# Attention of a hybrid block: unnormalised exponentials, three rounded value products, head outputs scaled by rows of inverse sums that go through DRAM

## The chip, the cores and the metric

One core of a Trainium2 chip runs the whole program. The metric is device microseconds of one execution, from start to end; lower is better. All inputs lie in DRAM as float32, and the output is float32.

## What is computed

The reference is one layer of a network on 512 tokens of width 1024 with a context of 256 more: a feed-forward sublayer, a mixer (a gated delta rule over 8 heads in both directions, and a softmax attention with 8 query heads over 2 key and value heads), and a second feed-forward sublayer. The change touches the attention alone, for 512 queries over 768 keys, 128 wide:

```python
def _attend(q, k, v):
    b, lq = q.shape[:2]
    qg = q.reshape(b, lq, ATTN_KV_HEADS, ATTN_GROUP, ATTN_DH)
    s = jnp.einsum('bqkgd,bskd->bkgqs', qg, k).astype(jnp.float32) * (ATTN_DH ** -0.5)
    p = jax.nn.softmax(s, axis=-1).astype(v.dtype)
    o = jnp.einsum('bkgqs,bskd->bqkgd', p, v)
    return o.reshape(b, lq, ATTN_Q)
```

## The kernel before, in words

The program is written by hand for each engine. Every engine runs its own list in order: SP loads weights, GpSimd (POOL) does some sums and DMAs, ScalarE (ACT), VectorE (DVE) and TensorE (PE) do the rest. Engines wait for each other by counting semaphores, `wait_ge` in front of an instruction and `then_inc` behind it. Nothing reorders the lists, so the order of the work is the order of the code.

Most matrix products are made as three products of operands that are rounded to the format fp32r: a value x is kept as x_hi (rounded, copied by ACT) and x_lo = x - x_hi (subtracted by DVE), and hi x hi, hi x lo and lo x hi are added up in PSUM. The feed-forward layers, the projections and the attention's scores are made so. The attention's value products are plain fp32 products.

PSUM has 8 banks of 512 columns. In the attention banks 4 to 7 hold scores (two banks for even tiles, two for odd ones), banks 0 and 1 the transposed probabilities of one tile, and banks 2 and 3 the outputs of an even and an odd head.

The attention goes over 32 tiles, i = 4n + t: head n of 8, and in it the block t of 128 queries. Their steps are interleaved:

- PE (lines 3161 to 3204): `scores(i + 2)`, six products of 384 columns, once the exponential of tile i is done; then six transposes of tile i, 128 keys each, of the normalised probabilities; then `weigh(i - 1)`, six fp32 products of 128 columns.
- DVE (lines 2407 to 2428): the maximum of tile i (L2417), its scaling by -1/sqrt(128) (L2420), then `normalise(i - 1)`: a reciprocal of the row's sum (L2410) and the scaling of 768 columns (L2412).
- ACT (lines 1509 to 1536): the exponential of tile i with its sum (L1522), then `evac_pt(i - 1)`, the copy of the 768 transposed columns to SBUF (L1512), and for t = 2 the copy of the last head's output (L1518).

Into the first tiles falls other work: the last query item is rotated and split (`item_rotate`, `item_hi`, `item_low`, lines 2307 to 2329 and 1445), and the values are turned by PE (L3146) and copied by ACT (L1505). At the end PE waits for all 8 heads (L3207) and goes on with the projections of the delta rule, `dn_gemm(0, 0)` to `dn_gemm(0, 2)` (L3407). POOL also waits for all heads (L854), then clears `d_s` and `d_up` (L856, L858); ACT and DVE wait for that before their part of the delta rule (L1695, L2436).

## Time and profile before

| what | value |
|---|---|
| time, median of 3 runs | 1834.33 us (1832.84 to 1838.05) |
| the profiled execution's own time | 1840.07 us |
| its span, first to last instruction | 1838.4 us |
| mean granted clock of TensorE | 0.996 |
| busy: PE, DVE, ACT, POOL | 97%, 67%, 52%, 22% of the span |
| attention, first reduction to first product behind it | 687.42 to 787.74 us |

All rows further down come from the profiled execution. A row of the timeline gives start and length in us, engine, line of the kernel, operation, output and inputs by the program's names, and in brackets how long the engine idled before it and who released it. Rows of the same kind that follow each other are merged (x6: six instructions). PE's matmuls overlap: the start of the next one tells the pace, not the length. `PE` rows of an fp32 product count twice (x12 for six products).

### The profile page before, as it was taken

What the parts mean: (1) busy time and instruction counts of PE and PEld (TensorE: products, weight loads), DVE (VectorE), ACT (ScalarE), POOL (GpSimd) and SP (SyncE); (2) the same over time, 40 slices, a digit from 0 to 9 for tenths busy, and PEclk for the clock granted to TensorE, in tenths of its full rate; (3) what the DMA queues carried; (4) which work ended last, traced back from release to release, by engine and by line L of the source; (5) the groups of instructions that cost most, each with busy time, mean ns of one, the idle gap of its engine ahead of it and who ended that gap; (6) DMA issues with size and microseconds to landing.
All of it is one profiled execution on the core that took longest, in us unless ns stands there. A gap on an engine that the chain in (4) does not pass through costs nothing.

```text
span 1838.4 us, 31419 instructions
## 1 busy us (share of the span) xinstructions
PE 1783.9 (97%) x11197; PEld 1657.6 (90%) x11197; DVE 1234.2 (67%) x2451; ACT 953.1 (52%) x1910; POOL 402.9 (22%) x296
## 2 busy tenths in 40 slices
PE   8899999999998999999999999999999999999997
PEld 5899999999997889999999999987889888898997
DVE  7768787868757666556777877765334675375576
ACT  6534242424446656565666666654223675464453
POOL 0714141313200120023232213310000052341330
PEclk9999999999999999999999999999999999999999
DMA  8133324454241430021222221122224112223232
GB/s 330 64 131 125 129 104 159 165 185 159 86 161 41 137 109 26 1 64 47 69 77 65 77 77 52 46 63 80 102 92 172 47 69 104 81 92 116 92 116 69
DMA packets 85142, 182.88 MB, mean 99 GB/s; under 512 B 33572, under 2 KB 42916, under 8 KB 84912
## 3 DMA queue, kind: packets, MB, share of 16 engines
q1 hardware_dynamic: 79584, 167.45, 26.4%
q0 software_dynamic: 3280, 13.95, 2.3%
q8 instruction: 63, 1.03, 0.2%
q10 hardware_dynamic: 2176, 0.13, 0.1%
q14 instruction: 39, 0.32, 0.1%
HBM read 169.91 MB, written 7.39 MB: 96 GB/s over the span
## 4 chain that ended last, share of the span: by engine, by line
PE 78%; DVE 7%; ACT 5%; issue 4%; POOL 2%; DMA 2%; SPq 2%; ACTq 0%; DVEq 0%; POOLq 0%
PE ps L2744 54%; PE ps L2955 15%; PE ps L3042 3%; PE ps L2748 3%; DMA raw<-W 1%; PE ps L3199 1%; ACT e_hi L1294 1%; DVE e_lo L2103 1%; SPq L748 1%; PE ps L3366 1%; PE ps L3328 1%; ACT ps L1279 1%; DVE ps L2145 1%; DVE w_lo L1993 0%; PE ps L3238 0%
## 5 line engine op out<-in xcount | busy, mean ns | idle before, releaser
L2744 PE MATMUL ps<-h_hi,w_hi 128*128 128x384 f32 (+2 forms) x720 | 240.9, 372 | 8.0 <-DVE h_lo L1879 3.4
L2744 PE MATMUL ps<-h_lo,w_hi 128*128 128x384 f32 (+2 forms) x720 | 237.7, 362 | 0.0
L2744 PE MATMUL ps<-h_hi,w_lo 128*128 128x384 f32 (+2 forms) x720 | 228.8, 357 | 0.0
L1809 DVE TENSOR_TENSOR w_lo<-raw,w_hi 128x1024 fp32r<-128x1024 f32 (+1 forms) x98 | 124.5, 1271 | 120.1 <-ACT w_hi L966 120.0
L966 ACT ACTIVATE w_hi<-raw 128x1024 fp32r<-128x1024 f32 (+1 forms) x106 | 111.3, 1050 | 146.8 <-PE ps L2744 144.9
L2744 PEld LDWEIGHTS ps<-h_hi,w_hi 128*128 128x128 f32 x720 | 130.8, 189 | 29.1 <-DVE h_lo L1879 8.0
L2744 PEld LDWEIGHTS ps<-h_lo,w_hi 128*128 128x128 f32 x720 | 133.5, 189 | 12.7 <-issue 1.2
L2744 PEld LDWEIGHTS ps<-h_hi,w_lo 128*128 128x128 f32 x720 | 133.3, 188 | 12.6
L2744 PE MATMUL ps<-g_hi,w_hi 128*128 128x384 f32 (+2 forms) x444 | 132.9, 346 | 0.8 <-DVE w_lo L1809 0.5
L2744 PE MATMUL ps<-g_lo,w_hi 128*128 128x384 f32 (+2 forms) x444 | 131.7, 343 | 0.0
L2744 PE MATMUL ps<-g_hi,w_lo 128*128 128x384 f32 (+2 forms) x444 | 131.7, 343 | 0.0
L3042 PE MATMUL ps<-f_hi,e_hi 128*128 128x256 f32 x356 | 102.1, 287 | 7.9 <-ACT f_pb L1338 3.9
L2955 PE MATMUL ps<-h_lo,w_hi 128*128 128x384 f32 x320 | 107.0, 334 | 2.2 <-ACT pb L1224 2.2
L2955 PE MATMUL ps<-h_hi,w_hi 128*128 128x384 f32 x320 | 107.3, 335 | 0.4 <-DVE ps L2033 0.3
L2955 PE MATMUL ps<-h_hi,w_lo 128*128 128x384 f32 x320 | 106.9, 334 | 0.0
L2955 PE MATMUL ps<-x_lo,w_hi 128*128 128x384 f32 x320 | 106.9, 334 | 0.0
L3042 PE MATMUL ps<-f_hi,e_lo 128*128 128x256 f32 x356 | 100.6, 283 | 0.0
L815 POOL TENSOR_TENSOR sums<-raw 128x512 f32<-128x512 f32 x20 | 28.9, 1444 | 278.6 <-DVE w_lo L1993 181.7
L2744 PEld LDWEIGHTS ps<-g_hi,w_hi 128*128 128x128 f32 x444 | 81.5, 188 | 7.4 <-DVE Y L2091 1.0
L2744 PEld LDWEIGHTS ps<-g_hi,w_lo 128*128 128x128 f32 x444 | 81.7, 188 | 5.0
L2744 PEld LDWEIGHTS ps<-g_lo,w_hi 128*128 128x128 f32 x444 | 81.7, 188 | 5.0
L1993 DVE TENSOR_TENSOR w_lo<-sums,w_hi 128x512 fp32r<-128x512 f32 x80 | 59.9, 753 | 33.8 <-ACT w_hi L1184 33.1
(478 smaller groups left out, 5112.9 us busy)
## 6 DMA issues: line engine op xcount, KB each, us to landing
raw<-W SPq DMA_DIRECT2D x221, 512.0 KB, 3.3
w_mod<-WMOD SPq DMA_DIRECT2D x68, 512.0 KB, 3.4
g_row<-g_rows POOLq DMA_DIRECT2D x8, 768.0 KB, 4.5
X<-XT SPq DMA_DIRECT2D x4, 768.0 KB, 7.1
d_matrices<-d_l SPq DMA_DIRECT2D x8, 384.0 KB, 2.8
a_sw<-i_n POOLq DMA_DIRECT2D x40, 64.0 KB, 1.9
w_first<-WMOD SPq DMA_DIRECT2D x4, 512.0 KB, 11.0
X<-XT SPq DMA_DIRECT2D x1, 2048.0 KB, 14.1
```

Of the source, the lines that this page charges most:

```text
L748: sp.dma_start(d_s[lv][r:r + b, :, col:col + b], d_l[r:r + b, 0, :, col:col + b]).then_inc(s("d_levels"), 16)
L815: g.tensor_tensor(s1[:], b1, b2, ALU.add).then_inc(s("s_add"), 1)
L966: a.activation(hi, src, ACT.Copy).then_inc(s("w_hi"), 1)
L1279: a.activation(copy_bank(pos), weight_part2(q, pos), ACT.Copy)
L1294: a.activation(slot2(True, q, pos), weight_part2(q, pos), ACT.Copy).then_inc(s("u_hi"), 1)
L1809: v.tensor_tensor(lo, src, hi.bitcast(F32), ALU.subtract).then_inc(s("w_split"), 1)
L1993: v.tensor_tensor(slot_of(w_lo, n, None), weight_part(q, pos), slot_of(w_hi, n, None).bitcast(F32), ALU.subtract)\
L2103: v.tensor_tensor(slot2(False, q, pos), src, slot2(True, q, pos).bitcast(F32), ALU.subtract).then_inc(s("u_lo"), 1)
L2744: return pe.matmul(out, lhsT, rhs, start=start, stop=stop)
L2748: return pe.matmul(out, lhsT, rhs, start=False, stop=True, skip_group_check=True)
L2955: last = pe.matmul(out_, slot_of((w_hi, w_hi, w_lo)[i], n + pos, k), (hi, lo, hi)[i][pos][:, k], start=pos in (A11, A12, S3) and k == 0 an ...
L3042: last = pe.matmul(out_, w[i][:, k], (hi, lo, hi)[i][:, k], start=pos in (A11, A12, S3) and k == 0 and i == 0, stop=True, skip_group_check ...
```

## The change

Five things change, all in the attention.

1. The exponentials are not normalised. PE transposes them as they come, three in bank 0 and three in bank 1, each bank with its own semaphore step.
2. ACT copies each bank's 384 columns as `p_hi` (`evac_hi`), and DVE subtracts that from PSUM into `p_lo` (`evac_low`). The values are split likewise: `v_hi` by ACT, `v_lo` by DVE (`value_low`).
3. The value products are made for two tiles together: a block `weigh(p, b)` handles the three key blocks of bank b for the pair p of tiles, with three fp32r products of 256 columns each. In tile i PE does `weigh(i // 2 - 1, i % 2)`, and after the last tile two blocks more.
4. After a head's four tiles DVE makes the reciprocals of its 4 x 128 sums (`recip`). POOL stores them as a row of 512 numbers in DRAM and loads that row into all 128 partitions (`a_r`); DVE multiplies the head's output by it (`out_head`), three tiles later.
5. PE waits for seven heads only before `dn_gemm(0, 0)`, and for the eighth before `dn_gemm(0, 2)`.

The diff, cut to its core:

```diff
         a_kc = at("a_kc", 204, [HKV, CTX])
-        a_v = at("a_v", 187, [NCH, HKV, P])
+        v_hi = at("v_hi", 187, [NCH, HKV, P], F32R)
+        v_lo = at("v_lo", 174, [NCH, HKV, P], F32R)
         i_raw = [at(f"i_raw{i}", 147 + 16 * i, [T]) for i in range(2)]
...
         a_p = at("a_p", 200, [2, T])
-        a_pt = [at("a_pt0", 147, [NCH, SEQ]), at("a_pt1", 159, [NCH, SEQ])]
-        a_m = at("a_m", 183, [3, 4])
+        p_hi = [at(f"p_hi{i}", 147 + 12 * i, [NCH, 2 * P], F32R) for i in range(2)]
+        p_lo = [at(f"p_lo{i}", 153 + 12 * i, [NCH, 2 * P], F32R) for i in range(2)]
+        a_m = at("a_m", 183, [4, 8])
+        a_r = [at(f"a_r{i}", 193 + 2 * i, [SEQ]) for i in range(2)]
         ba = at("ba", 184, [T])
...
             return ps[:, b, 0:(CTX, SEQ)[seg]]
+        def turned(b):
+            return ps[:, b, 0:3 * P].rearrange("p (c n) -> p c n", c=3)
+        def turned_to(t, i, b):
+            return t[i // 2 % 2][:, 3 * b:3 * b + 3, P * (i % 2):P * (i % 2) + P]
+        def head_bank(n):
+            return ps[:, 3 - n % 2, :]
         def solver_out(i):
...
             g.wait_ge(s("cb_loaded"), 16)
+            for n in range(H):
+                g.wait_ge(s("at_sum"), 2 * N_ITEM + n + 1)
+                g.dma_start(DL[0, 4 * n:4 * n + 4, :].rearrange("t q -> q t"), a_m[:, 3, 4 * (n % 2):4 * (n % 2) + 4], allow_slow_non_contiguous=True).then_inc(s("rows_stored"), 16)
+                g.wait_ge(s("rows_stored"), 32 * n + 32)
+                g.wait_ge(s("o_at"), n)
+                g.dma_start(a_r[n % 2][:], DL[0:1, 4 * n:4 * n + 4, :].rearrange("b t q -> b (t q)").to_broadcast([P, SEQ])).then_inc(s("rows_stored"), 16)
+                g.wait_ge(s("rows_stored"), 32 * n + 48)
             g.wait_ge(s("o_at"), H + 1)
...
                 a.wait_ge(s("at_vt"), j + 1)
-                a.activation(a_v[:, :, j, :].rearrange("p (b c) n -> p b c n", b=2),
+                a.activation(v_hi[:, :, j, :].rearrange("p (b c) n -> p b c n", b=2),
                              ps[:, 2 * j:2 * j + 2, 0:384].rearrange("p b (c n) -> p b c n", c=3), ACT.Copy).then_inc(s("at_vc"), 1)
-            def evac_pt(i):
-                a.wait_ge(s("at_tr"), i + 1)
-                t = i % 4
-                a.activation(a_pt[i // 4 % 2][:, :, P * t:P * t + P].rearrange("p (b c) n -> p b c n", b=2),
-                             ps[:, 0:2, 0:384].rearrange("p b (c n) -> p b c n", c=3), ACT.Copy)\
-                 .then_inc(s("at_pt"), 1)
-            def out_head(n):
-                a.wait_ge(s("at_pv"), n + 1)
-                a.activation(o_at[:, n, :], ps[:, 2 + n % 2, 0:SEQ], ACT.Copy).then_inc(s("o_at"), 1)
+            def evac_hi(i):
+                if i % 2 == 0 and i >= 4:
+                    a.wait_ge(s("at_pv"), i // 2 - 1)
+                if i == 2:
+                    a.wait_ge(s("at_rot"), N_ITEM)
+                for b in range(2):
+                    a.wait_ge(s("at_tr"), 2 * i + b + 1)
+                    a.activation(turned_to(p_hi, i, b), turned(b), ACT.Copy).then_inc(s("at_pt"), 1)
             for i in range(4 * H):
-                t = i % 4
                 a.wait_ge(s("at_max"), 2 * i + 2)
+                if i >= 8 and i % 4 == 0:
+                    a.wait_ge(s("at_sum"), 2 * N_ITEM + i // 4 - 1)
                 a.activation(a_p[:, i % 2, :].rearrange("p (b n) -> p b n", b=2),
                              ps[:, 4 + 2 * (i % 2):6 + 2 * (i % 2), 0:384],
-                             ACT.Exp, bias=a_m[:, 1, t:t + 1], scale=DH ** -0.5,
-                             accum_out=a_m[:, 2, t:t + 1]).then_inc(s("at_p"), 1)
+                             ACT.Exp, bias=a_m[:, 1, i % 8:i % 8 + 1], scale=DH ** -0.5,
+                             accum_out=a_m[:, 2, i % 8:i % 8 + 1]).then_inc(s("at_p"), 1)
                 if i == 0:
                     for j in range(HKV):
                         value_tokens(j)
                 if i:
-                    evac_pt(i - 1)
+                    evac_hi(i - 1)
                 if i == 1:
                     item_hi(N_ITEM - 1)
-                if i >= 4 and t == 2:
-                    out_head(i // 4 - 1)
-            evac_pt(4 * H - 1)
-            out_head(H - 1)
+            evac_hi(4 * H - 1)
             def take(b):
...
                     v.tensor_copy(g_out[0:96, :], ps[0:96, 6, 0:P]).then_inc(s("gates_v"), 1)
-            def normalise(i):
-                t = i % 4
-                v.wait_ge(s("at_p"), i + 1)
-                v.reciprocal(a_m[:, 2, t:t + 1], a_m[:, 2, t:t + 1]).then_inc(s("at_pn"), 1)
-                v.wait_ge(s("at_pn"), 2 * i + 1)
-                v.tensor_scalar(a_p[:, i % 2, :], a_p[:, i % 2, :], a_m[:, 2, t:t + 1], None, ALU.mult)\
-                 .then_inc(s("at_pn"), 1)
+            def value_low(j):
+                v.wait_ge(s("at_vc"), 2 * j + 1)
+                v.wait_ge(s("at_vt"), HKV)
+                v.tensor_tensor(v_lo[:, :, j, :].rearrange("p (b c) n -> p b c n", b=2),
+                                ps[:, 2 * j:2 * j + 2, 0:384].rearrange("p b (c n) -> p b c n", c=3),
+                                v_hi[:, :, j, :].rearrange("p (b c) n -> p b c n", b=2).bitcast(F32), ALU.subtract).then_inc(s("at_vc"), 1)
+            def evac_low(i):
+                for b in range(2):
+                    v.wait_ge(s("at_pt"), 2 * i + b + 1)
+                    v.tensor_tensor(turned_to(p_lo, i, b), turned(b), turned_to(p_hi, i, b).bitcast(F32), ALU.subtract).then_inc(s("at_pl"), 1)
+            def recip(n):
+                v.wait_ge(s("at_p"), 4 * n + 4)
+                if n >= 2:
+                    v.wait_ge(s("rows_stored"), 32 * (n - 2) + 32)
+                c = slice(4 * (n % 2), 4 * (n % 2) + 4)
+                v.reciprocal(a_m[:, 3, c], a_m[:, 2, c]).then_inc(s("at_sum"), 1)
+            def out_head(n):
+                v.wait_ge(s("at_pv"), 2 * n + 2)
+                v.wait_ge(s("rows_stored"), 32 * n + 48)
+                v.tensor_tensor(o_at[:, n, :], head_bank(n), a_r[n % 2][:], ALU.mult).then_inc(s("o_at"), 1)
             for i in range(4 * H):
-                t = i % 4
+                c = i % 8
                 v.wait_ge(s("at_s"), i + 1)
-                v.tensor_reduce(out=a_m[:, 0, t:t + 1], in_=ps[:, 4 + 2 * (i % 2):6 + 2 * (i % 2), 0:384],
+                v.tensor_reduce(out=a_m[:, 0, c:c + 1], in_=ps[:, 4 + 2 * (i % 2):6 + 2 * (i % 2), 0:384],
                                 op=ALU.max, axis=AX.XY).then_inc(s("at_max"), 1)
                 v.wait_ge(s("at_max"), 2 * i + 1)
-                v.tensor_scalar(a_m[:, 1, t:t + 1], a_m[:, 0, t:t + 1], -DH ** -0.5, None, ALU.mult)\
+                v.tensor_scalar(a_m[:, 1, c:c + 1], a_m[:, 0, c:c + 1], -DH ** -0.5, None, ALU.mult)\
                  .then_inc(s("at_max"), 1)
+                if i == 0:
+                    for j in range(HKV):
+                        value_low(j)
                 if i:
-                    normalise(i - 1)
+                    evac_low(i - 1)
                 if i == 1:
                     item_rotate(N_ITEM - 1)
                 if i == 2:
                     item_low(N_ITEM - 1)
-            normalise(4 * H - 1)
+                if i and i % 4 == 0:
+                    recip(i // 4 - 1)
+                if i > 4 and i % 4 == 3:
+                    out_head(i // 4 - 1)
+            recip(H - 1)
+            evac_low(4 * H - 1)
+            out_head(H - 1)
             def bc(x):
...
                 last.then_inc(s("at_s"), 1)
-            def weigh(i):
-                n, t = i // 4, i % 4
-                pe.wait_ge(s("at_pt"), i + 1)
-                if t == 0 and n >= 2:
+            def turn(i):
+                pe.wait_ge(s("at_p"), i + 1)
+                for b in range(2):
+                    if i:
+                        pe.wait_ge(s("at_pl"), 2 * i - 1 + b)
+                    for c in range(3):
+                        last = pe.transpose(ps[:, b, P * c:P * c + P], a_p[:, i % 2, P * (3 * b + c):P * (3 * b + c + 1)], ident)
+                    last.then_inc(s("at_tr"), 1)
+            def weigh(p_, b):
+                n = p_ // 2
+                pe.wait_ge(s("at_pl"), 4 * p_ + 3 + b)
+                if p_ % 2 == 0 and b == 0:
                     pe.wait_ge(s("o_at"), n)
-                for c in range(NCH):
-                    last = mm(ps[:, 2 + n % 2, P * t:P * t + P], a_v[:, c, n // 4], a_pt[n % 2][:, c, P * t:P * t + P],
-                              c == 0, c == NCH - 1)
-                if t == 3:
+                for c in range(3 * b, 3 * b + 3):
+                    for i, (v_, x) in enumerate(((v_hi, p_hi), (v_hi, p_lo), (v_lo, p_hi))):
+                        last = mm(head_bank(n)[:, 2 * P * (p_ % 2):2 * P * (p_ % 2) + 2 * P], v_[:, c, n // 4], x[p_ % 2][:, c],
+                                  c == 0 and i == 0, c == NCH - 1 and i == 2)
+                if b:
                     last.then_inc(s("at_pv"), 1)
...
                     scores(i + 2)
-                pe.wait_ge(s("at_pn"), 2 * i + 2)
-                if i:
-                    pe.wait_ge(s("at_pt"), i)
                 if i == 0:
-                    pe.wait_ge(s("at_vc"), HKV)
-                for c in range(NCH):
-                    last = pe.transpose(ps[:, c // 3, P * (c % 3):P * (c % 3) + P],
-                                        a_p[:, i % 2, P * c:P * c + P], ident)
-                last.then_inc(s("at_tr"), 1)
-                if i:
-                    weigh(i - 1)
-            weigh(4 * H - 1)
-            pe.wait_ge(s("o_at"), H + 1)
+                    pe.wait_ge(s("at_vc"), 2 * HKV)
+                turn(i)
+                if i >= 2:
+                    weigh(i // 2 - 1, i % 2)
+            for b in range(2):
+                weigh(2 * H - 1, b)
+            pe.wait_ge(s("o_at"), H)
             def merge_gemm(it, j):
...
             dn_gemm(0, 1)
+            pe.wait_ge(s("o_at"), H + 1)
             dn_gemm(0, 2)
```

DVE's order in the middle of the attention, before (`a_m` holds maxima, scaled maxima and sums, `a_p` the probabilities, `ps` is PSUM):

```order
L2417 TENSOR_REDUCE a_m<-ps 128x1 [waits at_s]
L2420 TENSOR_SCALAR a_m<-a_m 128x1 [waits at_max]
L2410 RECIPROCAL a_m<-a_m 128x1 [waits at_p]
L2412 TENSOR_SCALAR a_p<-a_p,a_m 128x768 [waits at_pn]
L2417 TENSOR_REDUCE a_m<-ps 128x1 [waits at_s]
```

Now, at the end of one head and the start of the next:

```order
L2449 TENSOR_REDUCE a_m<-ps 128x1 [waits at_s]
L2452 TENSOR_SCALAR a_m<-a_m 128x1 [waits at_max]
L2433 TENSOR_TENSOR p_lo_141<-ps,p_hi_139 128x3x128 [waits at_pt] x2
L2445 TENSOR_TENSOR o_at<-ps,a_r_143 128x512 [waits rows_stored,at_pv]
L2449 TENSOR_REDUCE a_m<-ps 128x1 [waits at_s]
L2452 TENSOR_SCALAR a_m<-a_m 128x1 [waits at_max]
L2433 TENSOR_TENSOR p_lo_141<-ps,p_hi_139 128x3x128 [waits at_pt] x2
L2440 RECIPROCAL a_m<-a_m 128x4 [waits at_p]
```

The reciprocal and scaling that waited for an exponential (`at_p`) have given way to two subtractions that wait for ACT's copies (`at_pt`), ahead of the next reduction. The head's product also waits for POOL's DMA (`rows_stored`).

ACT's order at the same place, before:

```order
L1522 ACTIVATE a_p,a_m<-ps,a_m 128x768 [waits at_max]
L1512 ACTIVATE a_pt_138<-ps 128x6x128 [waits at_tr]
L1518 ACTIVATE o_at<-ps 128x512 [waits at_pv]
L1522 ACTIVATE a_p,a_m<-ps,a_m 128x768 [waits at_max]
L1512 ACTIVATE a_pt_138<-ps 128x6x128 [waits at_tr]
```

and now:

```order
L1541 ACTIVATE a_p,a_m<-ps,a_m 128x768 [waits at_max]
L1536 ACTIVATE p_hi_139<-ps 128x3x128 [waits at_tr] x2
L1541 ACTIVATE a_p,a_m<-ps,a_m 128x768 [waits at_max]
L1536 ACTIVATE p_hi_138<-ps 128x3x128 [waits at_tr,at_pv]
L1536 ACTIVATE p_hi_138<-ps 128x3x128 [waits at_tr]
```

The copies of a tile still stand behind the exponential of the next one; there are two instead of one, and the head's copy is gone.

## Rows read from the trace of the kernel before

**Rows 1.** The page: busy time of each engine
```profile
PE 1783.9 (97%) x11197; PEld 1657.6 (90%) x11197; DVE 1234.2 (67%) x2451; ACT 953.1 (52%) x1910; POOL 402.9 (22%) x296
```

**Rows 2.** Busy times of three tiles' time: us, then busy us (x instructions) of each engine
```profile
700.00:709.12 9.12, 9.12 (x74) 9.02 (x74) 5.41 (x12) 5.24 (x9) 0.00 (x0) 1.00 0.00 0
```

**Rows 3.** Who waited for whom, 686 to 788 us: total, times, longest
```profile
DVE a_m L2417 <- PE ps L2744: 32.5, 28, 1.2
```

**Rows 4.** Timeline, one tile: start us, us, engine line op, out<-in, count
```profile
723.53 0.59 PE L2744 MATMUL ps<-k_hi,q_hi 128*128 128x384 f32 x2
...
724.66 0.82 PE L3199 MATMUL ps<-ca,a_p 128*128 128x128 f32 x6
...
724.86 0.96 DVE L2417 TENSOR_REDUCE a_m<-ps 128x1 f32<-128x768 f32 x1 [1.17 <-PE ps L2744]
...
725.31 1.50 PE L2744 MATMUL ps<-a_pt,a_v 128*128 128x128 f32 x12
...
725.85 0.16 DVE L2420 TENSOR_SCALAR a_m<-a_m 128x1 f32<-128x1 f32 x1
...
726.22 0.90 ACT L1522 ACTIVATE a_p<-ps,a_m 128x768 f32<-128x768 f32 x1
...
726.57 0.59 PE L2744 MATMUL ps<-k_hi,q_hi 128*128 128x384 f32 x2
```

**Rows 5.** Timeline, the first tiles of the attention
```profile
687.42 0.95 DVE L2417 TENSOR_REDUCE a_m<-ps 128x1 f32<-128x768 f32 x1
...
688.59 0.90 ACT L1522 ACTIVATE a_p<-ps,a_m 128x768 f32<-128x768 f32 x1 [1.59 <-DVE a_m L2420]
...
689.48 1.50 ACT L1505 ACTIVATE a_v<-ps 128x768 f32<-128x768 f32 x2
...
690.35 0.68 DVE L2315 TENSOR_TENSOR a_t<-i_n,cb 128x512 f32<-128x512 f32 x1
...
690.95 0.69 DVE L2317 TENSOR_TENSOR a_t<-a_sw,cb 128x512 f32<-128x512 f32 x1
...
692.28 0.95 DVE L2417 TENSOR_REDUCE a_m<-ps 128x1 f32<-128x768 f32 x1
```

**Rows 6.** One line's instructions: duration ns min/median/max
```profile
L976 ACT ACTIVATE v_raw<-ps x4: 470/476/483, 679.1 to 686.5; 128x384 f32<-128x384 f32 x4
```

**Rows 7.** Timeline, elsewhere: two subtractions on DVE; two 256-column products
```profile
100.65 0.55 DVE L2026 TENSOR_TENSOR pa<-ps,pa 128x384 f32<-128x384 f32 x1
...
101.12 0.95 DVE L2019 TENSOR_TENSOR g_lo<-ps,g_hi 128x768 fp32r<-128x768 f32 x1
...
101.99 0.68 DVE L1993 TENSOR_TENSOR w_lo<-raw,w_hi 128x512 fp32r<-128x512 f32 x1
...
1640.24 0.28 PE L3042 MATMUL ps<-f_hi,e_lo 128*128 128x256 f32 x1
...
1640.36 0.28 PE L3042 MATMUL ps<-f_hi,e_hi 128*128 128x256 f32 x1
```

**Rows 8.** Timeline, the end of the attention and what follows
```profile
779.58 0.96 DVE L2417 TENSOR_REDUCE a_m<-ps 128x1 f32<-128x768 f32 x1 [1.17 <-PE ps L2744]
...
787.74 0.50 PE L2744 MATMUL ps<-h_hi,w_hi 128*128 128x512 f32 x1 [0.69 <-ACT o_at L1518]
...
789.42 0.74 POOL L858 MEMSET d_up<- 128x772 f32 x1
...
793.53 0.60 ACT L1699 ACTIVATE d_up<-ps 128x512 f32<-128x512 f32 x1 [3.04 <-PE ps L2744]
```

**Rows 9.** DMA issues of the page: KB each, us to landing
```profile
g_row<-g_rows POOLq DMA_DIRECT2D x8, 768.0 KB, 4.5
...
d_b<-d_matrices SPq DMA_DIRECT2D x8, 48.0 KB, 2.0
```

**Rows 10.** Timeline, slack in the first head of the delta rule
```profile
811.17 0.63 DVE L2459 TENSOR_SCALAR d_c<-d_up,hn 128x770 f32<-128x770 f32 x1 [1.28 <-ACT d_up L1546]
```

**Rows 11.** Busy times in the second FFN, columns as in rows 2, then PEclk
```profile
1660.00:1680.00 20.00, 17.87 (x141) 16.97 (x140) 14.89 (x24) 11.82 (x25) 4.74 (x4) 1.00 0.40 135
```

## Prediction

> **What bounds the kernel now.** I read the page first. It shows a kernel in which TensorE's matmuls fill the span [rows 1], which says nothing yet of the stage that changes. The windows in the middle of the attention are plainer: 9.12 us of 9.12 are busy on PE, 5.41 on DVE and 5.24 on ACT, at a granted clock of 1.00, the 2.4 GHz level [rows 2]. 9.12 us are three tiles (a tile is 128 queries of one head; there are 32), so one takes 3.04. The waits agree: DVE's reduction waits for PE's scores before 28 of the 32 tiles, 32.5 us in all [rows 3], and no wait of PE of that size stands there. The timeline splits the 3.04 us [rows 4]: scores from 723.53 to 724.66 (1.13), six transposes to 725.31 (0.65), value products to 726.57 (1.26). PE is the bound, and DVE and ACT each idle over 3 of every 9 us. A product saved on PE pays only while DVE and ACT can follow. Busy times alone do not tell that: the order in their queues does.
>
> **The change on PE.** Six fp32 value products of a tile (twelve PE instructions, 1.26 us) become nine products of 256 columns. Such products follow each other every 0.12 us (1640.24 to 1640.36) [rows 7], so 9 x 0.12 = 1.08. PE's tile costs 1.13 + 0.65 + 1.08 = 2.86, 0.18 less; that is 5.8 us in 32 tiles, if PE stays the bound.
>
> **The change on DVE and ACT.** DVE loses a scaling of 768 columns and a reciprocal, and gets two subtractions of 384 columns per tile, one reciprocal and one product of 512 columns per head. ACT's one copy of 768 becomes two of 384, and its head copy goes. As busy time both still fit under 2.86 us. But look at what waits for what in the new order:
> - DVE, tile i: reduce i, scale i, then the two subtractions of tile i-1, which wait for ACT's copies of tile i-1;
> - ACT, tile i: exponential i, which waits for scale i, and only then the copies of tile i-1;
> - DVE's reduce i+1 stands behind those subtractions.
>
> So reduce i, scale i, exponential i, copies i-1, subtractions i-1, reduce i+1 is one closed chain through two queues, and each tile runs it once. Before, DVE's second half of tile i needed only exponential i-1, long done, and the copies were in nobody's way. The chain's price:
> - reduce start to exponential start, 687.42 to 688.59: 1.17 [rows 5];
> - exponential start to the next ACT instruction, 688.59 to 689.48: 0.89 [rows 5];
> - first copy of 384 columns from PSUM, 0.476 [rows 6], and 0.04 for the handover (a reduce ends at 724.86 + 0.96 = 725.82 and the scale that waits for its semaphore starts at 725.85 [rows 4]; I round up): 0.52. The second copy runs beside the first subtraction;
> - two subtractions: after one of 384 columns the next DVE instruction starts 0.47 later (100.65 to 101.12), although the instruction lasts 0.55 [rows 7]: 0.94.
>
> Sum 3.52 us per tile, over PE's 2.86 and over the present 3.04. PE is not in the chain: scores i+1 start when exponential i-1 is done, 1.13 + 0.65 later transposes i-1 are issued, and ACT comes to copy them only 3.52 + 0.89 after the start of exponential i-1.
>
> **One place where the skill differs.** The pair of rows above has the next instruction start 0.08 us before the subtraction's end [rows 7], and I count the start distance. The Trainium skill, VectorE: DVE Perf Modes, section "The TRN2 errata — SBUF-src ops pay a fixed extra latency per instruction", gives an fp32 tensor_tensor (N+151)/0.96 ns, 557 ns at 384 columns, and says that this latency is exposed between instructions; by it the chain would be 2 x 0.09 longer and the result an estimated 5.4 us later. This trace agrees with the 0.55 as a duration and not as a distance.
>
> **Per head** the chain also carries, between subtractions and next reduce, the reciprocal (0.15, like the small scaling of rows 4) and the head's product of 512 columns (0.60, from 690.35 to 690.95) [rows 5].
>
> **The sum**, from reduce 0, which nothing earlier moves:
> - Reduce 0 to 1: exponential 0 starts at 1.17, the value copies at 2.06; the second subtraction of v_lo starts at 2.91 + 0.87 = 3.78 (the first waits for one copy, 0.8; 768 columns take 0.87, 101.12 to 101.99 [rows 7]) and reduce 1 at 4.65.
> - Reduce 1 to 2: the chain, 3.52, and the rotation of the last item, 690.35 to 692.28, 1.93 [rows 5]: at 10.10.
> - Reduce 2 to 3: 3.52 and q_lo, 0.60: at 14.2.
> - Reduce 3 to 31: 28 x 3.52 = 98.6, seven reciprocals 1.05, six head products 3.6: at 117.4.
> - Before, reduce 31 came 779.58 - 687.42 = 92.2 after reduce 0 [rows 5, 8]. That is +25.2.
> - Tail: before, 8.16 from reduce 31 to the first product of the delta rule at 787.74 [rows 8]. Now the subtractions of tile 30 end at 3.6, the last transposes are issued by 4.0, three blocks of nine products take 3.24, and the wait is for the seventh head alone: 7.2. That is -0.9.
>
> **Sum +24.3 us.** The profiled execution took 1840.07 us (span 1838.4), 5.7 above the median of 1834.33; the difference is applied to the median: 1858.6.
>
> **What I cost at nothing, and its cover.** The row of inverse sums goes out to DRAM and back. DVE needs it three reductions after the reciprocal, 3 x 3.52 = 10.6 us later. The trace has no store of 4-byte pieces. From below: 768 pieces of 64 B landed in 2.0 us [rows 9], and a 256 KB load lies between that and the 768 KB one of 4.5 [rows 9], so 2.0 + 2.6 = 4.6. From above: both at twice the first and at the second, 4.0 + 4.5 = 8.5, plus up to 1 us of issue. I take 6, since counts of pieces resemble the first row. All are below 10.6, so nothing waits; from there on each microsecond counts in seven heads. For the last head the cover is PE's: the first two blocks of the delta rule use no bank of that head; the first takes 5.8 us (787.74 to 793.53) [rows 8], the second has 48 products of 384 columns at 1.13 / 6 [rows 4], 9 us. POOL's clearing of d_up now follows this product: reciprocal done at 4.3, row at 10.3, product at 11.1, and as before 2.5 us to the clearing's end (789.42 + 0.74, 2.4 after the start at 787.74): 13.5, or 6.3 after PE's start. ACT first needs it 5.8 after (793.53) [rows 8]. These 0.5 us vanish in the slack further on, where DVE idled 1.28 [rows 10]; at a trip of 9.5 us some 2 us would remain.
>
> **Rivals.**
> 1. *PE stays the bound, no slowdown.* If the handovers overlapped enough for the chain to fall from 3.52 + 0.19 (the head's share) to 2.86, the stage would be 14.2 + 28 x 2.86 = 94.3 against 92.2, less 0.9: +1.2 us, 1835.5. For it: DVE and ACT are busy only 60% now. Against it: each link is a measured duration of this stage or its shape, and 0.85 us per tile would have to vanish. It decides (less than 5.5 us over before) from about 3.0 down, the head's share included.
> 2. *The row comes late.* With a trip of 15 us, DVE waits 4.4 us in front of seven products: +31, 1889. For it: 512 separate 4-byte writes per head, of which there is no row. Against: [rows 9].
> 3. *TensorE's clock falls.* PE would be busy 2.86 of 3.7 us instead of all the time. At the 1.2 GHz level its tile is 5.7 us and becomes the bound: 32 x (5.7 - 3.04) = +85, 1919. Against it: with 17.87 of 20 us busy, in pieces, the clock stood at 1.00 [rows 11]; a share of 77% has no row. The Trainium skill, TensorE: Matmul & The Clock Gate, part 1, says that idling throttles the array to 1.2 GHz; no run here shows how much idling that takes.
> 4. *The change does not use its new products*: excluded, since the diff's loops over plain numbers make all 18 per pair of tiles.
>
> **How the numbers follow.** The closed chain 0.87; rival 1, 0.04; rival 2, 0.06; rival 3, 0.03. The prediction is 1858.6 us. Low end: each of the two subtractions 0.07 shorter and the run at the fast end (1832.84), -4.5 - 1.5: 1852. High end: subtractions at their full 0.55 (+4.9), the late clearing (+2), waits for two semaphores and the slow end of the runs (+3): 1869. About 0.3% is what a measurement of this kernel can tell from no change. Slower 0.93, within 0.3% 0.04 (rival 1), faster 0.03 (rival 1 with cheaper products than rows 7 show).
>
> **What would show it.** Right: reductions about 3.5 us apart, 4.1 where a head's product lies between; ACT's copies starting as soon as the exponential lets them, not when the transposes end; PE idle some 0.8 us per tile in front of scores; the inverse rows landing before DVE asks. Wrong: PE busy throughout (rival 1), DVE waiting on a DMA at the head's product (rival 2), PEclk near 0.5 (rival 3).

## The result, and the profile after

The changed kernel takes **1897.74 us** (median of six runs, 1896.54 to 1900.15) against 1834.91 for the kernel before in the same comparison (1832.84 to 1839.77): ratio 1.0339, 95% interval 1.0324 to 1.0354, or 62.8 us slower. Forecast were 1858.6 us and a range of 1852 to 1869. The direction was right; of the increase I had seen 24 us of 63, and the time lies far outside the range. The profiled execution of the changed kernel took 1897.12 us.

The page of the changed kernel. First its head line and the busy times, to be held against [rows 1]; then the slices with TensorE's granted clock, the chain of work that ended last (shares of the span), and two of the DMA issues (engine's queue, count, KB each, median us from issue to landing):

```profile
span 1895.1 us, 31340 instructions
...
PE 1794.0 (95%) x11101; PEld 1662.9 (88%) x11101; DVE 1245.7 (66%) x2469; ACT 950.6 (50%) x1934; POOL 413.0 (22%) x312
...
PE   8899999999998987678999999999999999999997
...
PEclk9999999999999998899999999999999999999999
...
PE 63%; DVE 10%; DMA 9%; ACT 7%; issue 5%; SPq 3%; POOL 2%; DVEq 0%; ACTq 0%; POOLq 0%
...
a_r<-d_matrices POOLq DMA_DIRECT2D x8, 256.0 KB, 4.7
...
d_matrices<-a_m POOLq DMA_DIRECT2D x8, 2.0 KB, 8.8
```

The busy times of DVE, ACT and POOL hardly moved. What is new sits in three places: PE's busy slices fall to 6 to 8 tenths in the attention, the clock row has two 8s there, and 9% of the chain now runs through DMA, where it was 2%. The two DMA rows give the reason away at once. The row of inverse sums, 2 KB, takes 8.8 us to be stored, nearly twice as long as the 256 KB that are read back. The next view, who waited for whom from 680 to 860 us in the changed kernel (total, times, longest), says who pays:

```profile
ACT a_p L1541 <- DVE a_m L2452: 84.4, 32, 7.3
...
POOL a_r L872 <- DMA d_matrices<-a_m: 67.7, 8, 9.2
DVE p_lo L2433 <- ACT p_hi L1536: 46.0, 31, 2.5
DVE o_at L2445 <- DMA a_r<-d_matrices: 41.1, 8, 13.6
...
PE ps L2785 <- ACT a_p L1541: 34.9, 13, 5.8
```

[Rows 3] had DVE waiting for PE before 28 tiles. Nothing of that is left. DVE now waits for ACT's copies in 31 tiles (the chain that was forecast, 1.5 us each) and for the row from DRAM at all eight head products: 41.1 us in all, 13.6 of them for the last head, so 27.5 for the seven others, 3.9 each. The forecast had no wait there.

One head on DVE, in the timeline of the changed kernel (start, length, what it waited for):

```profile
747.49 0.17 DVE L2440 RECIPROCAL a_m<-a_m 128x4 f32<-128x4 f32 x1
747.57 0.93 DVE L2449 TENSOR_REDUCE a_m<-ps 128x1 f32<-128x768 f32 x1
...
751.06 0.95 DVE L2449 TENSOR_REDUCE a_m<-ps 128x1 f32<-128x768 f32 x1
...
754.60 0.95 DVE L2449 TENSOR_REDUCE a_m<-ps 128x1 f32<-128x768 f32 x1
...
757.18 1.02 DVE L2433 TENSOR_TENSOR p_lo<-ps,p_hi 128x384 fp32r<-128x384 f32 x2 [1.44 <-ACT p_hi L1536]
763.00 0.69 DVE L2445 TENSOR_TENSOR o_at<-ps,a_r 128x512 f32<-128x512 f32 x1 [4.80 <-DMA a_r<-d_matrices]
763.61 0.95 DVE L2449 TENSOR_REDUCE a_m<-ps 128x1 f32<-128x768 f32 x1
```

and the same trip on POOL:

```profile
748.21 0.76 POOL L869 DMA_DIRECT2D d_matrices<-a_m  x1 [8.97 <-DVE a_m L2440]
757.44 0.54 POOL L872 DMA_DIRECT2D a_r<-d_matrices  x1 [8.47 <-DMA d_matrices<-a_m]
```

The reductions are 3.49 and 3.54 us apart where no wait for a row lies between them; 3.52 was forecast. The reciprocal starts at 747.49, the store is issued at 748.21 and has landed by 757.4, the load is issued at 757.44, and the product can start at 763.00: a trip of 15.5 us. Without the wait the product would have started at 763.00 - 4.80 = 758.20, so the cover was 10.7 us, and 10.6 was forecast. Everything on DVE stands behind that product, so 4.8 us of waiting delay the reduction at 763.61, and with it the exponential, the scores and PE.

Where the seven waits end, the last head begins its own:

```profile
837.91 0.17 DVE L2440 RECIPROCAL a_m<-a_m 128x4 f32<-128x4 f32 x1
...
852.60 0.69 DVE L2445 TENSOR_TENSOR o_at<-ps,a_r 128x512 f32<-128x512 f32 x1 [13.62 <-DMA a_r<-d_matrices]
...
855.01 0.73 POOL L879 MEMSET d_up<- 128x772 f32 x1
...
855.78 0.31 ACT L1712 ACTIVATE ones_r<-ca 128x128 fp32r<-128x128 f32 x1 [21.01 <-POOL d_up L879]
...
857.62 1.23 DVE L1825 TENSOR_TENSOR w_lo<-raw,w_hi 128x1024 fp32r<-128x1024 f32 x1 [1.24 <-ACT w_hi L987]
```

Product, POOL's clearing of `d_up`, ACT's first instructions and DVE's next weights follow one another; PE, which began the delta rule at 840.82, then waits 4.15 us at 858.95 for those weights. ACT's start of the delta rule was forecast 6.3 us after PE's; it came 855.78 - 840.82 = 15.0 after.

The first reduction of the attention stands where it stood, at 687.46 (before 687.42 [rows 5]). The first product of the delta rule has gone from 787.74 [rows 8] to 840.82. So 53.0 us of the increase lie between the two. DVE's copy of the delta rule's first head shows what follows, first in the kernel before and then now:

```profile
864.27 0.69 DVE L2475 COPY d_o<-ps 128x512 f32<-128x512 f32 x1 [2.19 <-PE ps L2748]
```
```profile
840.82 0.40 PE L2785 MATMUL ps<-h_hi,w_hi 128*128 128x512 f32 x1
...
925.10 0.69 DVE L2516 COPY d_o<-ps 128x512 f32<-128x512 f32 x1 [2.19 <-PE ps L2789]
```

It came 76.5 us after the first product and now comes 84.3 after it, which adds 7.7: 60.7 up to there. The medians are 62.8 apart. The two profiled executions as a whole differ by only 57.0 (1897.12 and 1840.07), because behind this copy that of the kernel before takes 4.1 us longer (974.1 against 970.0) in code that the change does not touch. So the 60.7 are an account of the stage, and the whole agrees with them within a few us, not better.

The granted clock is the last thing to read. Busy time by windows of the changed kernel (us, then PE, PEld, DVE, ACT and POOL busy with their counts, granted clock, DMA share, GB/s):

```profile
686.00:726.00 40.00, 26.79 (x170) 24.55 (x168) 22.14 (x40) 16.66 (x36) 1.90 (x3) 0.91 0.14 40
726.00:766.00 40.00, 27.22 (x169) 26.15 (x170) 18.51 (x38) 15.26 (x35) 2.60 (x4) 0.86 0.09 14
766.00:806.00 40.00, 29.47 (x178) 27.92 (x179) 19.93 (x41) 14.80 (x35) 3.35 (x5) 0.84 0.07 14
```

and PE's first instructions after one of the waits, in the timeline:

```profile
746.19 1.01 PE L2785 MATMUL ps<-k_hi,q_hi 128*128 128x384 f32 x2 [4.75 <-ACT a_p L1541]
...
748.27 1.48 PE L3218 MATMUL ps<-ca,a_p 128*128 128x128 f32 x6
```

PE is busy two thirds to three quarters of the time at 0.84 to 0.91 of full clock, where [rows 2] have 1.00. After an idle time of 4.75 us its two score products take 1.01 us instead of 0.59 and the six transposes 1.48 instead of 0.82 [rows 4]. From 746.2 to 750 us the granted clock is 0.50, the lower level of 1.2 GHz.

### The profile page after: what moved, and what is told of

The parts are those of the page before. It is cut to its first block, busy times and chain, and to the rows that moved or that the text cites. A ratio compares the mean times of both kernels' runs of the same rounds, so it can differ in the third digit from the quotient of the medians.

```text
span 1895.1 us, 31340 instructions
## 1 busy us (share of the span) xinstructions
PE 1794.0 (95%) x11101; PEld 1662.9 (88%) x11101; DVE 1245.7 (66%) x2469; ACT 950.6 (50%) x1934; POOL 413.0 (22%) x312
## 3 DMA queue, kind: packets, MB, share of 16 engines
q8 instruction: 62, 1.02, 0.2%
## 4 chain that ended last, share of the span: by engine, by line
PE 63%; DVE 10%; DMA 9%; ACT 7%; issue 5%; SPq 3%; POOL 2%; DVEq 0%; ACTq 0%; POOLq 0%
PE ps L2785 43%; PE ps L2996 14%; DMA d_matrices<-a_m 4%; PE ps L2789 3%; SPq L761 2%; DMA a_r<-d_matrices 2%; PE ps L3083 2%; DMA d_xc<-d_b 1%; DMA raw<-W 1%; ACT e_hi L1315 1%; DVE e_lo L2119 1%; DMA d_matrices<-d_l 1%; PE ps L3412 1%; ACT ps L1300 1%; ACT d_qu L1625 1%
```

## The experiments

After the result the working theory was: the chain costs what was forecast, the trip's excess over its cover costs seven times some 4 us, and the last head the rest. The rivals: that the slower clock or the DMA traffic, and not the wait, holds the heads up; that the missing time sits elsewhere; and, for the store, that the queue and not the size of its pieces makes it slow.

**e1_no_row: the trip taken out.** POOL fills both row buffers with 1.0 once, and the heads stay unnormalised. DVE's products stay where they are.

```diff
-            for n in range(H):
-                g.wait_ge(s("at_sum"), 2 * N_ITEM + n + 1)
-                g.dma_start(DL[...].rearrange("t q -> q t"), a_m[...])
...
+            g.wait_ge(s("at_sum"), 2 * N_ITEM + 1)
+            for n in range(2):
+                g.memset(a_r[n][:], 1.0).then_inc(s("row_set"), 1)
...
-                v.wait_ge(s("rows_stored"), 32 * n + 48)
+                v.wait_ge(s("row_set"), 2)
```

> Leaves out: the rows of inverse sums do not go through DRAM and are not used; POOL fills the two row buffers with 1.0 once, and the product with the head's output stays, so that every engine's instructions are as in the change, only the trip is gone. The profile of the change shows reductions 3.54 us apart between the head products and DVE idle 4.0 us before seven of them for the DMA. Theory A (two separate costs: the closed chain through ACT and DVE, about 24 us; and the trip of 15 us against a cover of 10.6, about 28 us in seven heads and 8 us behind the last head): 1835 + 24 = 1859, chain still 3.54 us per tile, no wait for a DMA, clock 1.00. Rival B (TensorE's fallen clock, 0.84 to 0.91 in the stage, is what lengthens it, and the trip only coincides): over 1875, and the clock stays under 1. Rival C (the chain exists only because the waits let the engines fall out of step): about 1836.

Measured: 1862.83 us (1861.21 to 1864.48; ratio 1.0142, interval 1.0125 to 1.0159), against 1835.84 for the kernel before in this comparison: +27.0. Four tiles of its timeline on DVE:

```profile
736.65 0.95 DVE L2443 TENSOR_REDUCE a_m<-ps 128x1 f32<-128x768 f32 x1
...
740.25 0.93 DVE L2443 TENSOR_REDUCE a_m<-ps 128x1 f32<-128x768 f32 x1
...
743.74 0.94 DVE L2443 TENSOR_REDUCE a_m<-ps 128x1 f32<-128x768 f32 x1
...
747.25 0.95 DVE L2443 TENSOR_REDUCE a_m<-ps 128x1 f32<-128x768 f32 x1
...
750.76 0.68 DVE L2439 TENSOR_TENSOR o_at<-ps,a_r 128x512 f32<-128x512 f32 x1
751.36 0.94 DVE L2443 TENSOR_REDUCE a_m<-ps 128x1 f32<-128x768 f32 x1
```

3.60, 3.49, 3.51 and, over the head product, 4.11: 14.71 us for a head of four tiles, where the prediction's own terms give 4 x 3.52 + 0.75 = 14.83. The clock is at 1.00 from 710 to 780 us. In the first tiles it is not: from 700 to 710 us it is 0.66. There the fourth and fifth steps between reductions take 4.74 and 3.97 us. PE has waited 4.19 us for `q_lo`, begins scores 4 at 702.26 at the lower level, and reaches the transposes of tile 2 only at 704.35, so ACT's copies wait 1.00 us for them. In its profiled execution the first reduction starts at 687.81 and the delta rule at 813.37, 125.6 us, where the kernel before took 787.74 - 687.42 = 100.3: 25.2 longer. Behind that nothing is left: the copy of the first head comes 76.7 us later, as before (76.5). So the chain is shown with its size, and the other 36 us of the increase hang on the trip. The profiled executions as a whole are 24.4 us apart (1864.48 and 1840.07), so they do not account for all of the medians' 27.0.

**e2_late: the head's product two tiles later, the trip unchanged.**

```diff
-                if i > 4 and i % 4 == 3:
-                    out_head(i // 4 - 1)
+                if i > 8 and i % 4 == 1:
+                    out_head(i // 4 - 2)
+            out_head(H - 2)
```

> The head's product and its wait for the row stand two tiles later in DVE's list (after tile 4n+9 instead of 4n+7), with the trip as it is; all is computed. Cover before the product: 5 chains of 3.54 = 17.7 us against a trip of 15. Theory A: the waits of seven heads vanish except at the last head and at the seventh, which now comes after the last reduction; the stage loses about 26 us, the delta rule's delay behind the last head (8 us) stays: about 1869 to 1873. Rival B (clock): over 1885. Rival C: as now, 1897, if DVE's wait was only idle time that another wait takes over.

Measured: 1871.47 us (1869.36 to 1876.05; 1.0200, 1.0180 to 1.0221). Its DMA rows and its two waits for the row:

```profile
a_r<-d_matrices POOLq DMA_DIRECT2D x8, 256.0 KB, 4.5
d_matrices<-a_m POOLq DMA_DIRECT2D x8, 2.0 KB, 8.4
```
```profile
ACT ones_r L1712 <- POOL d_up L879: 19.3, 1, 19.3
...
DVE o_at L2445 <- DMA a_r<-d_matrices: 15.7, 2, 13.1
```

The store is as slow as in the change, but DVE waits for it only twice: 2.6 us for the seventh head, whose product the edit could not put any later, and 13.1 for the last. The increase over the kernel before falls from 62.8 to 35.6 us, by 27, and the waits in the heads by 27.5 - 2.6 = 24.9. What is left over e1_no_row, 8.6 us, is the last two heads' trips, which this edit doesn't cover: the attention is 2.1 us longer (686.49 to 814.18) and the delta rule's first head comes 84.0 us after its start instead of 76.7, as in the change (84.3). The same traffic with a longer cover costs nothing in the heads: it was the wait.

**e3_store16: the store in pieces of 16 bytes.** Each partition's four inverse sums go out as they lie. The load is unchanged, so the row's order is no longer that of the queries, and outputs are scaled by the wrong sums.

```diff
-  g.dma_start(DL[...].rearrange("t q -> q t"), a_m[:, 3, ...], allow_slow_non_contiguous=True)
+  g.dma_start(DL[...].rearrange("t (q c) -> (t q) c", c=4), a_m[:, 3, ...])
```

> The store of the inverse sums goes out as each partition's 16 contiguous bytes, 128 pieces in place of 512 pieces of 4 bytes, so the row's order is not the queries' and outputs are scaled by the wrong sums; the load and all waits are unchanged. Theory D (the many 4-byte pieces make the store's 8.8 us): the store lands in 2 to 3 us, the trip is about 7.5 to 8.5 us, under the cover of 10.6: no wait at any head, about 1859 to 1861. Rival E (it is the write to DRAM from POOL's queue as such): store stays near 8.8 us, time stays at 1897.

Measured: 1862.14 us (1860.00 to 1862.43; 1.0137, 1.0120 to 1.0154). Its DMA rows:

```profile
a_r<-d_matrices POOLq DMA_DIRECT2D x8, 256.0 KB, 3.5
d_matrices<-a_m POOLq DMA_DIRECT2D x8, 2.0 KB, 1.7
```

The same 2 KB on the same queue land in 1.7 us instead of 8.8. The last head's trip, whose end can be seen because DVE waits for it, is 7.0 us (reciprocal 810.21, product 817.16), near the 6 that I had taken. With it the kernel takes what it takes without any trip (e1_no_row, 0.7 us apart), the last head included. That is the world of the forecast: 26.3 us over the kernel before, where it had 24.3.

**e4_sp_store: the 4-byte store on SP's queue.** POOL keeps the load. The edit also puts two of SP's weight loads behind the stores.

```diff
+            for n in range(H):
+                sp.wait_ge(s("at_sum"), 2 * N_ITEM + n + 1)
+                sp.dma_start(DL[...].rearrange("t q -> q t"), a_m[...]).then_inc(s("sp_stored"), 16)
...
-                g.dma_start(DL[...].rearrange("t q -> q t"), a_m[...])
-                g.wait_ge(s("rows_stored"), 32 * n + 32)
+                g.wait_ge(s("sp_stored"), 16 * n + 16)
```

> The same store of 512 pieces of 4 bytes, issued from SP's queue instead of POOL's; all is computed. Theory D (pieces): it lands in 8 to 9 us as before, and the time stays within 5 us of 1897. Rival F (POOL's queue, whose descriptors are made by software, is slow with many pieces): it lands in 2 to 3 us like the 768 pieces of 64 bytes that SP stores elsewhere, and the time falls to about 1860.

Measured: 1888.58 us (1885.61 to 1890.93; 1.0280, 1.0263 to 1.0297). Its DMA rows and waits:

```profile
a_r<-d_matrices POOLq DMA_DIRECT2D x8, 256.0 KB, 4.0
d_matrices<-a_m SPq DMA_DIRECT2D x8, 2.0 KB, 8.4
```
```profile
DVE o_at L2450 <- DMA a_r<-d_matrices: 31.6, 8, 13.4
```

The store takes 8.4 us on the other queue too. Its small pieces make it slow, not the queue. Still the increase is 10.1 us smaller than the change's (52.7 against 62.8), where at most 5 had been expected. The waits of the seven heads fall from 27.5 to 31.6 - 13.4 = 18.2, which is 9.3 of them: SP issues the store 0.20 us after the reciprocal's start (761.93, 762.13), where POOL took 0.72, and the rest of the 1.3 us per head lies in the slightly shorter store and load (8.4 and 4.0 against 8.8 and 4.7). Past the point where the cover is used up, each microsecond of the trip counts seven times, as the prediction says. The expectation for this run speaks of 768 pieces of 64 bytes that SP stores; that row is a load from DRAM into SBUF (`d_b` is the output), so no row showed how fast SP stores small pieces.

**f1_row_fixed: the 16-byte store, and the row read in its new order.** This is e3_store16 with all of the computation in place.

```diff
-  v.tensor_tensor(o_at[:, n, :], head_bank(n), a_r[n % 2][:], ALU.mult)
+  v.tensor_tensor(o_at[:, n, :].rearrange("p (t q) -> p t q", t=4), head_bank(n).rearrange("p (t q) -> p t q", t=4),
+                  a_r[n % 2][:].rearrange("p (q t) -> p t q", t=4), ALU.mult)
```

> The store as each partition's 16 contiguous bytes, as in e3_store16, and DVE's product reads the loaded row with a step of four numbers, so that every query gets its own sum and all is computed. Theory A: the trip is 6 to 7 us and hidden, the closed chain stays at 3.54 us per tile: 1860 to 1863, as e3_store16. Rival (a read with a step of four costs DVE more): the product of 0.69 us grows, by up to 0.5 us in each of eight heads, 1866.

Measured: 1865.26 us (1864.25 to 1867.32; 1.0157, 1.0142 to 1.0173) against 1836.61 for the kernel before in this comparison. That is 2 us over what was expected, and the product's row shows why:

```profile
736.42 1.08 DVE L2445 TENSOR_TENSOR o_at<-ps,a_r 128x512 f32<-128x512 f32 x1
737.41 0.96 DVE L2450 TENSOR_REDUCE a_m<-ps 128x1 f32<-128x768 f32 x1
```

With one input read in steps of four numbers it lasts 1.08 us instead of 0.68, and 0.40 for each of seven heads on the chain is 2.8 us. It is a cheap repair all the same: 28.7 us over the kernel before instead of 62.8.

**f2_copies_first, f3_turn_first, f4_both: the order in the queues.** All three stand on f1_row_fixed. f2 issues ACT's copies of tile i-1 before the exponential of tile i:

```diff
+                if i:
+                    evac_hi(i - 1)
                 exponential i
-                if i:
-                    evac_hi(i - 1)
```

f3 issues PE's transposes of tile i before the scores of tile i+2; f4 has both.

> f1_row_fixed with ACT's two copies of tile i-1 ahead of exponential i in its list. That opens the chain reduce, exponential, copies, subtractions, but makes another through PE: exponential i, scores i+2 (1.13), transposes i (0.33 to the first bank's end, 0.49 with its drain, the second 0.33 later), copies i, exponential i+1: 0.98 + 1.13 + 0.82 + 0.48 = about 3.4 us per tile. Theory A: some 10 us below f1, about 1852. Rival G (the pace is not set by the order in the lists but by DVE's and ACT's busy time): no change from f1.

> f1_row_fixed with PE's transposes of tile i ahead of scores i+2. PE is not in the closed chain of f1, so theory A expects no change: 1860 to 1863. Rival H (PE's late transposes hold the copies back): clearly below f1, by up to 20 us.

> Both orders together: neither chain is left above PE's own 2.86 us per tile (scores 1.13, transposes 0.65, nine products 1.08). Theory A: PE is the bound again, tiles 2.87 us apart, the stage is some 27 us shorter than f1 and about 2 us shorter than before: 1833 to 1836. Rival G (busy time of DVE and ACT): at best 1852, as f2.

Measured: f2 1856.75 us (1852.76 to 1857.65; 1.0109, 1.0093 to 1.0124); f3 1863.24 (1861.35 to 1863.60; 1.0139, 1.0123 to 1.0155); f4 **1831.68** (nine runs, 1829.37 to 1834.79; 0.9973, 0.9963 to 0.9983). One order alone gives 8.5 us or 2.0; both give 33.6. f2 was expected at about 1852 and came 5 us later. Why it stops early is in its timeline, one round of ACT and PE:

```profile
749.08 0.62 PE L2786 MATMUL ps<-k_hi,q_hi 128*128 128x384 f32 x2 [0.44 <-ACT a_p L1543]
...
750.23 0.82 PE L3219 MATMUL ps<-ca,a_p 128*128 128x128 f32 x6
...
750.81 0.87 ACT L1536 ACTIVATE p_hi<-ps 128x384 fp32r<-128x384 f32 x2 [1.79 <-PE ps L3219]
...
751.57 0.91 ACT L1543 ACTIVATE a_p<-ps,a_m 128x768 f32<-128x768 f32 x1
...
752.62 0.61 PE L2786 MATMUL ps<-k_hi,q_hi 128*128 128x384 f32 x2 [0.51 <-ACT a_p L1543]
```

Scores, transposes behind them, copies, exponential behind the copies, next scores: 752.62 - 749.08 = 3.54 us. The edit opens the first closed chain and closes another of the same length, through PE and ACT. In f1_row_fixed this second chain has two tiles of time: the copies of tile i stand behind exponential i+1, so the path from exponential i over scores, transposes and copies leads to exponential i+2. With the copies first it leads to exponential i+1. What f2 saves is what DVE alone carries per head, the reciprocal and the product: a head takes 14.08 us between reductions instead of 15.12, and 7 x 1.04 = 7.3 of the 8.5.

f3 leaves the first chain closed, so its later tiles are as in f1. Its 2.0 us are small beside the intervals of f1 and f3, which overlap, but the timelines have a gain in the first tiles: the fourth and fifth steps between reductions take 3.52 and 3.60 us instead of 4.74 and 4.00, 1.6 us, because the transposes no longer wait behind scores 4. With both orders neither chain binds, and the busy times of f4_both from 710 to 780 us are:

```profile
710.00:780.00 70.00, 69.49 (x529) 69.28 (x528) 57.22 (x114) 45.00 (x102) 6.50 (x12) 1.00 0.10 24
```

PE is the bound again, at full clock, and its tile can be read from the transposes of two tiles in a row:

```profile
704.41 0.82 PE L3219 MATMUL ps<-ca,a_p 128*128 128x128 f32 x6
...
707.18 0.82 PE L3219 MATMUL ps<-ca,a_p 128*128 128x128 f32 x6
```

2.77 us, against 3.04 before and 2.86 forecast if PE stayed the bound. Of the 0.27, the value products make 0.20: nine take 1.06 us (706.12 to 707.18) where the twelve instructions took 1.26. The rest lies in the transposes, 0.58 instead of 0.65. That is 32 x 0.27 = 8.6 us less. Of these the attention keeps 4.9 (687.48 to 782.93, 95.4 us against 100.3), and the median 4.9: at its start PE waits 3.68 us for `v_lo`, at 692.39, and the second reduction comes at 692.25 instead of at 688.48. This version leaves nothing of the computation out and is 4.9 us, 0.3%, faster than the kernel before: the nine products of the change do pay, a little, once neither the row nor the order is in their way.

## Why the prediction was wrong

**What bounds the kernel now: right.** PE was the bound, its products were the saving, and what mattered was whether DVE and ACT could follow. f4_both shows the saving itself, slightly larger than forecast (2.77, not 2.86, per tile).

**The closed chain: right, in mechanism and in size.** 3.49 to 3.60 us between reductions (forecast 3.52), 4.11 over a head's product (forecast "4.1"), two subtractions counted by their start distance of 0.47 and not by their length: 750.61 to 751.55 in f1_row_fixed is 0.94 for both, although the pair lasts 1.02. Here the trace kept deciding against the estimate that was worked out from the Trainium skill, VectorE: DVE Perf Modes, section "The TRN2 errata — SBUF-src ops pay a fixed extra latency per instruction". The runs f1 to f4 add what the prediction did not say: the order that opens this chain on ACT closes another of 3.54 us through PE, and both orders together are needed.

**The sum, +24.3: right within 1 to 3 us.** Without any trip the stage is 25.2 us longer in the profiled execution, and the median 27.0; no run separates the 2 us between the two. Part of the closeness is luck, because two small errors cancel. The first tiles take 1.6 us more than the sum has (PE at the lower clock behind its wait for `q_lo`, and its transposes behind scores 4), and the heads take 14.71 us where the terms give 14.83.

**"What I cost at nothing, and its cover": the step that failed.** It took 6 us for the trip, between 4.6 and 8.5 (9.5 with issue); the trip is 15.5. Three terms were mis-sized. The store was priced by its count of pieces, from 768 pieces of 64 bytes in 2.0 us [rows 9]; its 512 pieces of 4 bytes took 8.8. That row is moreover no store but a load, from DRAM into SBUF on SP's queue. The load of the row was put at 2.6 us, between the 2.0 and the 4.5 of [rows 9]; it took 4.7, as long as the one with three times the bytes. And 2.0 us lie between the instructions and the transfers, where up to 1 was allowed. The cover was right (10.7, forecast 10.6), and so was the warning that each microsecond beyond it counts seven times. But the upper bound, "twice the first row", was no bound: nothing in the trace was of that kind, and I let a row of another kind close the range. The bound stood at 9.5 and the cover at 10.6; a bound only a little looser would have let the seven waits into the range.

**The last head: the same step.** The prediction said that at a trip of 9.5 us "some 2 us would remain". At the trip that came, 7.7 us remained.

Put together, from the profiled executions: 25.2 for the chain (e1_no_row), 27.8 for the heads' waits (53.0 - 25.2; DVE's own sum of seven waits is 27.5), 7.7 for the last head. That is 60.7. The medians say the same with other terms: 27.0 without a trip, 35.8 for the trip, of which e2_late leaves 8.6.

**The rivals.** Rival 2 is what happened: a trip of 15 us and waits of 4.4 before seven products were worked out at +31, and 15.5 and 3.9 came. It gave 1889; it lacks the last head's 7.7. I had given it 0.06 "against [rows 9]", which held no such store. Rival 1 was excluded by e1_no_row. Rival 3 was half seen: the clock did fall, to 0.84 in a stretch, but the fall does not come with the chain's own idle time. At about 0.7 us of that per tile it stood at 1.00 (e1_no_row, 710 to 780 us). It fell behind waits for the row that left PE idle for 4.75 to 5.79 us, and also without them in the first tiles: in e1_no_row it was 0.55 from 694.7 to 698 us, behind idle times of 1.0 to 1.4 us, and 0.66 from 700 to 710, behind one of 4.19. In f4_both it stood at 1.00 behind 3.68 us. So the length of the last idle time alone does not tell in these runs whether it falls. In the heads the slower clock seems to have cost next to nothing: behind a wait, where PE ran at the lower level, the reductions came 3.60 and 3.49 us apart (743.97, 747.57, 751.06), as in e1_no_row at full clock (736.65, 740.25, 743.74), and DVE's idle times alone make 27.5 of the 27.8. No run has the waits without the fall, so this is read, not tried.

## What to carry to other kernels

Price a transfer by its contiguous pieces and its direction before its bytes, and where the trace has no transfer of that kind, let the range run past the cover. A tiny row on the way through DRAM is a latency and deserves either a long cover or a better layout: four adjacent numbers per piece took 7 us off each trip, and a read in steps on DVE that undoes the order cost 0.4. And when engines pass work back and forth through in-order queues, write down every closed loop of waits, and write them down again for the order that is to repair the first. Here moving ACT's copies opened a loop of 3.5 us and closed another of 3.54 through PE, and alone it gave a quarter of what both orders gave.

## What the runs showed of the hardware that was not expected

- A store of 2 KB from 128 partitions to DRAM took 8.4 to 8.8 us in 512 pieces of 4 bytes, on POOL's queue and on SP's alike, and 1.7 to 1.9 us in 128 pieces of 16 bytes. Whether the number of pieces or their size counts, these runs can't separate; the 768 pieces of 64 bytes in 2.0 us [rows 9] are a load into SBUF, the other way.
- A load of one row of 2 KB into 128 partitions (256 KB) took 3.5 to 4.7 us; three times as much took 4.5 [rows 9]. It took 3.5 to 3.9 us behind the 16-byte store and 4.0 to 4.7 behind the 4-byte one.
- A product of 512 columns of fp32 on DVE with one input read in steps of four numbers took 1.08 us instead of 0.68.
- The granted clock stood at 0.84 to 0.91 in stretches of the changed kernel in which PE was idle for 4.75 to 5.79 us at a time, and at 1.00 in e1_no_row from 710 to 780 us, where PE idled about 0.5 to 1.1 us before each tile's scores. It also fell in e1_no_row, to 0.55 from 694.7 to 698 us, behind idle times of 1.0 to 1.4 us.
